# Query transposes of the attention layer by VectorE blocks and a DRAM scratch, scores of heads 0-3 a half step later

## What is computed

```python
def moba_mixer(h, w_qkv, q_gain, k_gain, w_o, pos):
    q, k, v = jnp.split(h @ w_qkv, 3, axis=-1)
    q = rope(rms_norm(q.reshape(B, S, A_HEADS, A_HEAD_DIM), q_gain), pos)
    k = rope(rms_norm(k.reshape(B, S, A_HEADS, A_HEAD_DIM), k_gain), pos)
    ...
    s_own = jnp.einsum('bhqd,bhkd->bhqk', q_c, k_own) * scale
    p = jax.nn.softmax(jnp.where(kpos <= qpos, s_own, NEG))
    out = jnp.einsum('bhqk,bhkd->bhqd', p, v_own)
    ...
    return o @ w_o
```

## Time and profile before

| | us |
|---|---|
| median of 3 runs | 657.42 (657.22 to 658.22) |
| the profiled execution's own time | 657.28 |
| its span | 655.5 |
| TensorE matmuls busy (PE) | 651.9 |
| TensorE weight loads busy (PEld) | 553.1 |
| VectorE busy (DVE) | 432.1 |
| ScalarE busy (ACT) | 333.3 |
| GpSimd busy (POOL) | 26.8 |

### The profile page before, as it was taken

The page is one execution under the profiler, slowest core; times in us unless marked ns, Lnnn a source line. Parts: engine busy times, 40 slices in busy tenths (PEclk is TensorE's granted clock), DMA queues, the critical chain, the costliest instruction groups (busy, mean ns, idle before and its releaser), DMA issues.

```text
span 655.5 us, 8596 instructions
## 1 busy us (share of the span) xinstructions
PE 651.9 (99%) x3228; PEld 553.1 (84%) x3228; DVE 432.1 (66%) x486; ACT 333.3 (51%) x436; POOL 26.8 (4%) x29
## 2 busy tenths in 40 slices
PE   9999999999999999999999999999999999999998
PEld 7888888888888888888888888888888888888887
DVE  6898656598776454556996765764559977744531
ACT  7877664565554333445446546544447655433320
POOL 0163000000000000000000000000000000000000
DMA  9965458587655558655667657658876865565500
GB/s 325 388 229 192 129 150 276 169 249 224 191 187 201 193 192 262 195 147 188 210 193 256 194 176 271 192 166 283 237 212 177 242 206 185 182 204 195 180 0 33
DMA packets 95086, 132.45 MB, mean 202 GB/s; under 512 B 3792, under 2 KB 54480, under 8 KB 95056
## 3 DMA queue, kind: packets, MB, share of 16 engines
q1 hardware_dynamic: 94768, 130.73, 62.2%
q0 software_dynamic: 288, 1.31, 0.5%
HBM read 126.26 MB, written 5.77 MB: 201 GB/s over the span
## 4 chain that ended last, share of the span: by engine, by line
PE 99%; DVE 0%; issue 0%
PE acc L558 19%; PE acc L556 19%; PE acc L557 19%; PE scr L651 11%; PE acc L651 11%; PE acc L656 6%; PE scr L656 6%; PE acc L704 1%; PE scr L558 1%; PE scr L557 1%; PE scr L556 1%; PE acc L610 1%; PE acc L616 1%; PE acc L606 1%; PE scr L717 1%; PE scr L728 1%
## 5 line engine op out<-in xcount | busy, mean ns | idle before, releaser
L1097 DVE TENSOR_TENSOR lo<-raw,hi 128x2048 fp32r<-128x2048 f32 x108 | 246.9, 2287 | 104.7 <-ACT hi L849 104.4
L849 ACT ACTIVATE hi<-raw 128x2048 fp32r<-128x2048 f32 x108 | 207.0, 1918 | 138.4 <-PE acc L558 136.2
L556 PE MATMUL acc<-hi,aT_hi 128*128 128x512 f32 x252 | 98.1, 389 | 0.0
L557 PE MATMUL acc<-lo,aT_hi 128*128 128x512 f32 x252 | 98.1, 389 | 0.0
L558 PE MATMUL acc<-hi,aT_lo 128*128 128x512 f32 x252 | 98.0, 389 | 0.0
L556 PE MATMUL acc<-hi,h_both 128*128 128x512 f32 x208 | 83.4, 401 | 0.0
L558 PE MATMUL acc<-hi,h_both 128*128 128x512 f32 x208 | 81.2, 390 | 0.0
L557 PE MATMUL acc<-lo,h_both 128*128 128x512 f32 x208 | 81.0, 389 | 0.0
L651 PE MATMUL scr<-h_both,hi 128*128 128x512 f32 x320 | 77.6, 391 | 0.0
L651 PE MATMUL acc<-h_both,hi 128*128 128x512 f32 x320 | 77.4, 391 | 0.0
L651 PEld LDWEIGHTS acc<-h_both,hi 128*128 128x128 f32 x320 | 58.6, 188 | 11.2
(11 more groups left out here) (142 smaller groups left out, 668.9 us busy)
## 6 DMA issues: line engine op xcount, KB each, us to landing
raw<-in_mlp_w SPq DMA_DIRECT2D x64, 1024.0 KB, 5.5
raw<-in_r_w_in SPq DMA_DIRECT2D x24, 1024.0 KB, 5.2
raw<-in_a_w_qkv SPq DMA_DIRECT2D x8, 1024.0 KB, 9.6
raw<-in_r_w_out SPq DMA_DIRECT2D x8, 1024.0 KB, 5.8
raw<-in_a_w_qkv SPq DMA_DIRECT2D x16, 256.0 KB, 6.3
raw<-in_a_w_o SPq DMA_DIRECT2D x4, 1024.0 KB, 4.9
x_rows<-stage_b SPq DMA_DIRECT2D x40, 64.0 KB, 1.8
stage_a<-x_rows SPq DMA_DIRECT2D x10, 256.0 KB, 2.9
```

The costliest lines, as they stand in the source:

```text
L556: nc.tensor.matmul(dst, a_hi, b_hi, start=first, stop=False)
L557: nc.tensor.matmul(dst, a_hi, b_lo, start=False, stop=False)
L849: nc.scalar.activation(hi[:, s, :], raw[:, s, :], ACT.Copy).then_inc(hi_ready, 1)
L1097: nc.vector.tensor_tensor(lo[:, s, :], raw[:, s, :], hi[:, s, :].bitcast(F32), ALU.subtract).then_inc(lo_ready, 1)
```

## The change

The four query pieces (0, 1, 4, 5: `TURNED`) are no longer transposed by TensorE. VectorE transposes their 32 x 32 blocks from `rot` into a new buffer `q_blocks` (`turn_q`, "B p", in half steps 5, 5, 13, 14). SP writes them to a new DRAM scratch `q_rows` (four DMAs of 64 KB each, `write_q`) and reads each back with one DMA of 256 KB into `q_half` (`read_q`). ScalarE copies that into `qkT` (`store_q`, "Q p", in half steps 12, 12, 18, 18). In the SP queue the writes of pieces 0 and 1 stand behind the load of chunk 8, their reads behind that of chunk 9, the writes of pieces 4 and 5 behind the first two loads of the output projection, and their reads right after. The key pieces stay as they were. Scores, exponentials and N of heads 0 to 3 move one half step later (S from 12, 13, 15, 17 to 13, 14, 16, 18), and so do the transposes of their probabilities (P from 14, 15, 17, 19 to 15, 16, 18, 20); everything of heads 4 to 7 and all A stay.

```diff
...
             at[4 * b + 3 + t] += [("rope", p), ("raw", p)]
             at[4 * b + 4 + t].append(("left", p))
             at[VAR_AT[p]].append(("var", p))
-            at[4 * b + 6 + t].append(("T", p))
+            if p in TURNED:
+                at[BLOCKS_AT[p]].append(("B", p))
+                at[COPY_AT[p]].append(("Q", p))
+            else:
+                at[4 * b + 6 + t].append(("T", p))
     at[SQUARE_AT].append(("square", 0))
     at[FACTORS_AT].append(("factors", 0))
     for i in range(4):
...
         at[O_AT[h]].append(("O", h))
     at[SCALES_AT].append(("scales", 0))
-    first = ["T", "square", "var", "rope", "factors", "low", "raw", "high", "left"]
-    early = ["scales", "rope", "high", "low", "N", "v", "raw", "left", "var", "T", "A", "P", "S", "E"]
+    first = ["T", "square", "var", "rope", "factors", "low", "raw", "high", "left", "B"]
+    early = ["scales", "rope", "high", "Q", "low", "N", "B", "v", "raw", "left", "var", "T", "A", "P", "S", "E"]
     late = ["N", "A", "S", "v", "high", "O", "P", "E", "low"]
     for k in range(SLOTS):
         first_to_last = first if k < EARLY else early if k < LATE else late
...
+TURNED = (0, 1, 4, 5)
+STORED = [p for p in range(8) if p not in TURNED]
+BLOCKS_AT = {0: 5, 1: 5, 4: 13, 5: 14}
+COPY_AT = {0: 12, 1: 12, 4: 18, 5: 18}
 VAR_AT = [9, 9, 8, 9, 12, 13, 16, 17]
 VAR_ORDER = [2, 3, 0, 1, 4, 5, 6, 7]
 SQUARE_AT = 6
 FACTORS_AT = 7
 SCALES_AT = 14
-S_AT = [12, 13, 15, 17, 20, 21, 22, 23]
-P_AT = [14, 15, 17, 19, 22, 23, 24, 25]
+S_AT = [13, 14, 16, 18, 20, 21, 22, 23]
+P_AT = [15, 16, 18, 20, 22, 23, 24, 25]
 A_AT = [20, 21, 21, 22, 24, 25, 26, 26]
 O_AT = A_AT
 V_AT = [19, 20, 23, 23]
...
 EARLY = 10
 LATE = 20
 SCHEDULE = attention_schedule()
+QKT_ORDER = [i for k in range(SLOTS) for what, i in SCHEDULE[k] if what in ("T", "Q")]
+QKT_NO = [QKT_ORDER.index(p) + 1 for p in range(8)]
 SQUARES_BEFORE = sum(what == "raw" for k in range(SQUARE_AT) for what, _ in SCHEDULE[k])
 POWER_NO = [VAR_ORDER.index(p) + 2 if VAR_ORDER.index(p) >= 4 else VAR_ORDER.index(p) + 1 for p in range(8)]
 NORM_POWER_NO = 5
...
 def program(nc, x_in, tables, a_w_qkv, a_w_o, r_w_in, r_w_out, mlp_w1, mlp_w2,
             out):
     x_rows = nc.dram_tensor("x_rows", (TURNS, TT, P, 4, P), F32, kind="Internal").ap()
+    q_rows = nc.dram_tensor("q_rows", (len(TURNED), P, 4, P), F32, kind="Internal").ap()
     z_rows = nc.dram_tensor("z_rows", (HR, TT, P, 4, P), F32, kind="Internal").ap()
     rope_a, rope_r, decay, causal, gcol_src, ident_src, xT_src = tables
     with ExitStack() as ctx:
...
         xT_rows = at("xT_rows", 24 * KB, [P, GAINS + KD * SEQ])
         gcol_0 = xT_rows[:, 0:GAINS].rearrange("p (i kt) -> p i kt", kt=KD)
         xT_in = xT_rows[:, GAINS:GAINS + KD * SEQ].rearrange("p (kt t) -> p kt t", t=SEQ)
+        q_half = at("q_half", 36 * KB, [P, TT, 512])
+        q_blocks = at("q_blocks", 40 * KB, [P, TT, 512])
         rot = at("rot", 44 * KB, [P, 2, 512])
         probs = at("probs", 48 * KB, [P, 3, 384])
         rope_in = at("rope_in", 61 * KB, [P, 6 * P])
...
         out_done = sem("out_done")
         last_columns_ready = sem("last_columns_ready")
         x_blocks_ready = sem("x_blocks_ready")
+        q_blocks_ready = sem("q_blocks_ready")
+        q_out = [sem(f"q_out{t}") for t in range(TT)]
+        q_in = [sem(f"q_in{t}") for t in range(TT)]
         x_out = [sem(f"x_out{t}") for t in range(TT)]
         xT_half_in = [sem(f"xT_half_in{t}") for t in range(TT)]
         out_quarter_ready = sem("out_quarter_ready")
...
                 for kt in kts:
                     sp.dma_start(tok_view(raw, c)[:, kt, :],
                                  qkv_w[QKV_ORDER[c // 2], c % 2][:, kt, :]).then_inc(part_in[c][kt], 16)
+
+            def write_q(p_i):
+                n, t = TURNED.index(p_i), p_i % 2
+                sp.wait_ge(q_blocks_ready, n + 1)
+                for i in range(4):
+                    rows = q_rows[n].rearrange("(j r) i c -> i r j c", j=4)[i]
+                    sp.dma_start(rows, q_blocks[32 * i:32 * i + 32, t, :].rearrange("p (j c) -> p j c", j=4)
+                                 ).then_inc(q_out[t], 16)
+
+            def read_q(p_i):
+                n, t = TURNED.index(p_i), p_i % 2
+                sp.wait_ge(q_out[t], 64 * (n // 2 + 1))
+                if n >= 2:
+                    sp.wait_ge(qkT_ready, QKT_NO[p_i - 4])
+                sp.dma_start(q_half[:, t, :], q_rows[n].rearrange("d i c -> d (i c)")).then_inc(q_in[t], 16)
             load_xT(0)
             load_parts(0, [0, 1])
...
             load_qkv(6)
             sp.dma_start(mask[:], causal).then_inc(mask_in, 16)
             sp.dma_start(gcol[:], gcol_src).then_inc(gcol_in, 16)
-            for c in range(7, 12):
+            for c in range(7, 9):
+                load_qkv(c)
+            for p_i in (0, 1):
+                write_q(p_i)
+            load_qkv(9)
+            for p_i in (0, 1):
+                read_q(p_i)
+            for c in range(10, 12):
                 load_qkv(c)
             for s, (n, kg) in enumerate(WO_ORDER):
                 load(C_WO // 4, s, tok_view, wo_w[n, kg])
+                if s < 2:
+                    write_q(4 + s)
+                if s == 1:
+                    for p_i in (4, 5):
+                        read_q(p_i)
             load_w1(0)
             load_w2(0)
             for c in range(8):
...
                     pe.wait_ge(rot_sum_ready, p_i + 1)
                 else:
                     pe.wait_ge(k_scaled, 2 * (p_i // 4) + p_i % 2 + 1)
-                if p_i == 0:
+                if p_i == STORED[0]:
                     pe.wait_ge(ident_in, 16)
-                if p_i >= 1:
-                    pe.wait_ge(qkT_ready, p_i)
+                else:
+                    pe.wait_ge(qkT_ready, QKT_NO[STORED[STORED.index(p_i) - 1]])
                 for h in range(4):
                     m = nc.tensor.transpose(scr[:, 0, h * P:(h + 1) * P],
                                             rot[:, p_i % 2, h * P:(h + 1) * P], ident[:])
...
             def scores(h):
-                pe.wait_ge(qkT_ready, 4 + 4 * (h // 4))
+                pe.wait_ge(qkT_ready, max(QKT_NO[4 * (h // 4):4 * (h // 4) + 4]))
                 if h >= 1:
                     pe.wait_ge(m_ready, h)
                 nc.tensor.matmul(scr[:, 2, 0:P], qkT[:, 0, h, 0:P], qkT[:, 1, h, 0:P],
...
             def store_qkT(p_i):
                 j, t = p_i // 2, p_i % 2
-                act.wait_ge(rotT_ready, p_i + 1)
+                act.wait_ge(rotT_ready, STORED.index(p_i) + 1)
                 nc.scalar.copy(qkT[:, j % 2, 4 * (j // 2):4 * (j // 2) + 4, t * P:(t + 1) * P],
                                scr[:, 0, :].rearrange("p (h t) -> p h t", t=P)
+                               ).then_inc(qkT_ready, 1)
+
+            def store_q(p_i):
+                n, j, t = TURNED.index(p_i), p_i // 2, p_i % 2
+                act.wait_ge(q_in[t], 16 * (n // 2 + 1))
+                nc.scalar.copy(qkT[:, 0, 2 * j:2 * j + 4, t * P:(t + 1) * P].rearrange("p h (i c) -> p h i c", i=4),
+                               q_half[:, t, :].rearrange("p (i h c) -> p h i c", i=4, h=4)
                                ).then_inc(qkT_ready, 1)
             def exponentials(h):
...
                         norm_squares(0)
                     elif what == "T":
                         store_qkT(i)
+                    elif what == "Q":
+                        store_q(i)
                     elif what == "v":
                         v_copy(i)
                     elif what == "E":
...
                     dve.wait_ge(tables_g_ready, 1)
                 if p_i == 2:
                     dve.wait_ge(tables_g_ready, 2)
-                if p_i >= 2:
-                    dve.wait_ge(rotT_ready, p_i - 1)
+                if p_i - 2 in TURNED:
+                    dve.wait_ge(q_blocks_ready, TURNED.index(p_i - 2) + 1)
+                elif p_i >= 2:
+                    dve.wait_ge(rotT_ready, STORED.index(p_i - 2) + 1)
                 sin_done = dv.mark(nc.vector.tensor_tensor(u4, raw4, sin, ALU.mult))
                 nc.vector.tensor_tensor(r4, raw4, cos, ALU.mult).then_inc(rope_read, 1)
                 dve.wait_ge(dv.sem, sin_done)
...
                 ur = stage_b[:, t, :].rearrange("p (h o d) -> p h o d", o=2, d=64)[:, :, ::-1, :]
                 rr = rot[:, t, :].rearrange("p (h o d) -> p h o d", o=2, d=64)
                 nc.vector.tensor_tensor(rr, rr, ur, ALU.add).then_inc(rot_sum_ready, 1)
+
+            def turn_q(p_i):
+                n, t = TURNED.index(p_i), p_i % 2
+                dve.wait_ge(rot_sum_ready, p_i + 1)
+                if n >= 2:
+                    dve.wait_ge(q_out[t], 64)
+                nc.vector.transpose(q_blocks[:, t, :].rearrange("p (j a c) -> p a j c", j=4, a=4),
+                                    rot[:, t, :].rearrange("p (a j c) -> p a j c", a=4, j=4)
+                                    ).then_inc(q_blocks_ready, 1)
```

(2 more changed lines are left out.)

## The result

The changed kernel takes 659.83 us (median of 7 executions, 658.86 to 661.33), the kernel before, run beside it on the same chip, 657.48 (7 executions, 657.22 to 658.43). The ratio is 1.0038, with a 95% interval of 1.0028 to 1.0048: slower, as forecast (658.9, range 656.6 to 660.8), by 2.35 us where 1.45 were forecast. The profiled execution of the changed kernel took 658.86 us with a span of 657.1, against 657.28 and 655.5: there the difference is 1.58.

What follows compares the result with a forecast made beforehand. TensorE bounds it, with VectorE hardly behind between 31 and 60 us; the 1.76 us saved is swallowed by a wait, half step 21 comes 1.45 us late: 657.42 + 1.45 = 658.87, given as 658.9, range 656.6 to 660.8.

Steps and rivals of the forecast that it cites:

- TensorE's gain: TensorE's queue: four groups of four transposes leave, 0.44 us each, 1.76 us (0.27%) the whole possible gain.
- VectorE: VectorE's queue: four block transposes at 0.605 us; first two fill idle time, last two add 1.21 us.
- The order: Half step 16: head 1's normalised probabilities end at 57.93, so TensorE waits 2.4 to 3.2 us before transposing them.
- The sum: From head 1's probability transposes at 58.07, plus 14.62, 2.73 and 1.0, half step 21 comes at 76.42, 1.45 us late.
- Beside the path: DMA and ScalarE: load 9 lands at about 40.1, reads about 41.5, query copies wanted about 43.0; no cost taken.
- Rival 2: Query reads land late, delaying ScalarE's copies and VectorE's chain; at a quarter of the loads' pace 660.4 us; chance 0.15.
- Rival 1: Half step 16: VectorE is done when TensorE arrives, so the whole 1.76 us is kept, 655.7 us; chance 0.11.
- 1.45 us stay: After half step 21 both programs are the same and TensorE-bound, so the 1.45 us delay lasts to the end.
- N2 62.6, in time: VectorE finishes head 2's normalised probabilities at 62.6, before TensorE wants them in half step 18 at 64.6.

Runs made afterwards that it cites:

- changed, again: The changed kernel run once more, unedited, for more executions of its pause: 660.36 us (6 executions), ratio 1.0032 to 1.0057 against the kernel before.

## Why the prediction was right, and where it was off

**TensorE's gain.** The page has the 16 transposes less that were forecast; their 0.44 us a group isn't measured by itself. None of it is left at half step 21, because it all lies ahead of the wait.

**VectorE.** The first two block transposes fell into the idle place, and the other two took 0.63 and 0.62 us from start to start; from var 4 to the end of N1 VectorE took 1.21 us more than before. Each one is paid at P1 at its 0.6 (B5 later: the wait fell by 0.6). By the 311 ns that the Trainium skill gives for one bf16 tile ("VectorE: DVE Perf Modes", The three transpose paths) it would have been 2.6 us worse, an estimate; four float32 tiles take 0.70 here, and the measurement decides.

**The order.** N1 was forecast to end at 57.93, as a reordering of entries whose lengths were known, plus 1.21: it ended at 57.9. P1 was forecast for 58.07 and began at 58.01. TensorE was to wait 2.4 to 3.2: the row says 2.8. The experiments show it: the shift alone makes 0.7; the two block transposes of the second pair then make the difference between 0.7 (pieces 0 and 1 only) and 2.8, 1.21 by their own time and 0.88 by T4 and T5 that TensorE no longer does, 2.09 in all, where 2.1 is measured.

**The sum.** Half step 21 was forecast for 76.42 and came at 76.31. The profiled execution is 1.58 above the one before, forecast 1.45. The 0.24 between the 1.34 of half step 21 and the 1.58 of the end is far behind it: near 489 us TensorE waits 0.4 us at L694 for VectorE's `h_both`, where the kernel before doesn't wait.

**Beside the path.** Load 9 forecast 40.1, came 40.1; the reads 41.5, came at 40.8 and 41.4; copies at 43.0, came at 43.01. Rival 2 (late queries) is out. T3's wait (0.8) and low 5's of 0.2 came as forecast and were swallowed. Rival 1 (VectorE keeps up) is out by 2.8 us.

**What was mis-sized** is the last step of the sum, that behind half step 21 both programs are the same and "1.45 us stay". On the median 2.35 came. Two things were put at nothing.

The first is the clock: the prediction read the wait as lost time only. Over 13 executions of the changed kernel five had a mean clock of 0.997 and took 661.15 to 661.68; the eight at 0.999 or above took 658.64 to 660.66. The medians of the two groups are 1.8 us apart, and 0.003 of 657 us is 2.0. It goes with the pause: of the kernel whose profile has a longest wait of 5.0 us all five executions lost clock, with 3.1 three of five, with 2.8 five of thirteen, with 2.2 none of five, and with less none. The profiled execution happened to be one without.

The second is a value far behind the change. The eight executions that kept the clock have a median of 659.5, still 0.6 above the forecast. The profiled execution of "changed, again" is one of them (659.82, 0.96 above the first one's 658.86), and TensorE's waits in it show where that went:

```profile
PEld acc L694 <- DVE h_both L1177: 1.2, 5, 0.3
```

That is 0.8 more than in the first one. L694 is the start of the last MLP, and what it waits for hangs on the read of the turned residual from DRAM. ScalarE's timeline there, in the first profiled execution of the changed kernel:

```profile
487.38 1.71 ACT L909 ACTIVATE h_both<-stage_a,gcol 128x256 fp32r<-128x256 f32 x4 [3.94 <-DMA stage_a<-x_rows]
```

In the kernel before the same instruction starts at 484.85, 2.5 us earlier. In all twelve profiled executions of the table the time behind half step 21 exceeds that of the kernel before by about the wait at L694: by 0.0 to 0.1 where it is 0, by 0.2 to 0.7 where it is 0.4 to 0.6, by 1.1 and 1.2 in the two where it is 1.2. Nine of the eleven with turned queries have the wait, the shift alone and the kernel before don't. Why the residual comes late there, and in some executions more than in others, no run shows; it stays open.

**Right for a partly lucky reason** was "N2 62.6, in time", and with it that T6 and T7 keep their cost. VectorE's part was right (N2 was done at 62.7). But the sum didn't look at GpSimd, whose power 7 was held up from 1.01 to 2.98 us; only its scaling, at 66.10, found a slot. In three neighbours of this schedule T7 did wait (3.1, 1.7 and 0.9 us), the first two for this reason. The term at nothing could have been read beforehand, from the scalings of 2.22 and 2.68 us in the trace of the kernel before.

## What to carry to other kernels

Work that leaves the bounding engine is a gain only up to the next value that another engine hands it just in time. Before moving 1.76 us away, list those values in order (here low 5, scaled keys, N1, scaled keys again) and, for each, what stands ahead of it in its producer's queue: a block transpose in an idle place cost nothing, the same one ahead of N1 cost its full 0.6 us, and moving the low part of 2.3 us out from in front of N1 (with the three low parts behind it) brought 2.6 us. The list doesn't end with the stage: one such value here lies 400 us behind the change. A long wait of TensorE may cost more than its length, as it may take the clock with it: here those of 2.8 us did in part of the executions, and that of 5.0 in all. And a place that looks level in one schedule may be held by a gap of 1 us on another engine, so try the neighbours before trusting it.

## What the runs showed of the hardware

- A GpSimd instruction that began inside a low part of VectorE (both operands in SBUF), or together with it, ended only 0.6 to 0.9 us behind it: it went from 1.01 to 2.98 us and from 1.04 to 2.91 and 3.19. A small VectorE instruction that began inside GpSimd's scaling ended with it: from 0.16 to 0.81 and 0.33. Moving two 2.3 us instructions by one half step was worth 3.2 us, and 4.1 on the medians with the clock that came back.
- The same pause of TensorE lowered its granted clock in some executions of one program and not in others: in 5 of 13 at 2.8 us, 3 of 5 at 3.1, all 5 at 5.0. A fall cost 1.8 us in the first, by the medians, and 2.5 in the profiled one of the last.
- In a full queue what stands ahead counts in a DMA's time: the load of chunk 9 took 5.6 us before, and 7.1 with the eight writes (0.5 MB) ahead of it. By "DMA: Bandwidth & Descriptors" of the Trainium skill (2.0 us plus bytes at 436 GB/s) 1 MB would be 4.4, an estimate; the trace disagrees while the queue is full.
